# Products with the weights' upper part first in every 3-pass tile, those with the lower part last

## The reference

```
for l in range(DEPTH):                                   # DEPTH = 2
    u = rms_norm(x, mix_norm_g[l]) @ w_in[l]             # one input projection, split among three groups
    y_mla = mla_group(...)                               # latent attention, 8 heads, causal
    y_ssm = mamba2_group(...)                            # state-space scan in chunks of 128
    y_lru = rglru_group(...)                             # gated linear recurrence
    y_mix = concat([rms_norm(y_mla), y_ssm, rms_norm(y_lru)])
    x = x + y_mix @ w_out[l]
    x = x + memory_cross_attention(rms_norm(x), rms_norm(mem), w_mq[l], w_mk[l], w_mv[l], w_mo[l])
    hm = rms_norm(x, mlp_norm_g[l]) @ w_mlp1[l]          # 1024 -> 4096
    x = x + jnp.square(jax.nn.relu(hm)) @ w_mlp2[l]      # 4096 -> 1024
return rms_norm(x, final_norm_g)
```

## Time and profile before

| what | value |
|---|---|
| median of 3 runs | 3390.11 us (3389.93 to 3394.16) |
| the profiled execution | 3385.11 us |
| its span, first to last instruction | 3383.4 us |
| PE busy | 3054.3 us, 90% of the span, 14184 matmuls |
| POOL busy | 1143.3 us, 34% |
| DVE busy | 1212.6 us, 36% |
| ACT busy | 702.3 us, 21% |
| mean granted TensorE clock | 0.97 of full speed |

### The profile page before, as it was taken

One profiled execution on the slowest core, in us unless ns is written; L12 is line 12 of the kernel. 1 busy time (PEld: TensorE's weight loads), 2 busy tenths in 40 slices (PEclk: granted clock), 3 DMA queues, 4 the chain that ended last, 5 costly groups with the idle time before them and its releaser, 6 DMA issues. The chain is left out here.

```text
span 3383.4 us, 35420 instructions
## 1 busy us (share of the span) xinstructions
PE 3054.3 (90%) x14184; PEld 2404.3 (71%) x14184; DVE 1212.6 (36%) x1195; ACT 702.3 (21%) x1143; POOL 1143.3 (34%) x598
## 2 busy tenths in 40 slices
PE   4888899989999999999878889998889999999996
PEld 3765557766678888888767555687668788888885
DVE  6365445303432222222254644451044222222223
ACT  3034552103211001010121345420031111111011
POOL 2221213562233334343233122235603334334341
PEclk8889999999999999999988899999999999999998
DMA  3000001121011111111110000111201111111111
GB/s 131 31 23 12 5 1 63 56 75 43 31 38 50 44 50 43 50 49 44 40 42 31 20 6 1 38 44 63 81 13 43 38 50 43 50 50 43 50 48 58
DMA packets 41927, 142.88 MB, mean 42 GB/s; under 512 B 7024, under 2 KB 9072, under 8 KB 41200
## 3 DMA queue, kind: packets, MB, share of 16 engines
q1 hardware_dynamic: 41840, 141.67, 12.4%
HBM read 135.89 MB, written 5.77 MB: 42 GB/s over the span
## 5 line engine op out<-in xcount | busy, mean ns | idle before, releaser
L474 POOL TENSOR_TENSOR wsp<-raw,ones 128x1024 fp32r<-128x1024 f32 x236 | 453.0, 1919 | 1688.7 <-PE ps L602 1620.7
L602 PE MATMUL ps<-hB,wsp 128*128 128x512 f32 x3840 | 875.6, 389 | 5.4 <-DVE hB L1451 3.3
L602 PEld LDWEIGHTS ps<-hB,wsp 128*128 128x128 f32 x3840 | 720.8, 188 | 156.4 <-ACT hB L1119 4.1
L602 PE MATMUL ps<-hA,wsp 128*128 128x512 f32 x2880 | 672.6, 395 | 61.0 <-POOL wsp L477 44.7
L602 PE MATMUL ps<-hm,wsp 128*128 128x512 f32 x3072 | 703.2, 390 | 26.6 <-DVE hm L1537 26.6
L602 PEld LDWEIGHTS ps<-hm,wsp 128*128 128x128 f32 x3072 | 575.3, 188 | 151.8 <-issue 32.9
L602 PEld LDWEIGHTS ps<-hA,wsp 128*128 128x128 f32 x2880 | 547.8, 191 | 184.2 <-POOL wsp L477 39.3
L477 POOL TENSOR_TENSOR wsp<-raw,wsp 128x1024 fp32r<-128x1024 f32 x236 | 575.4, 2438 | 18.5
L1547 DVE TENSOR_TENSOR x<-ps,x 128x1024 f32<-128x1024 f32 x128 | 156.7, 1224 | 501.1 <-PE ps L602 501.1
L1181 ACT ACTIVATE ss<-ss 128x1024 f32<-128x1024 f32 x32 | 34.0, 1062 | 918.6 <-DVE ss L1529 918.6
L763 PE MATMUL ps<-kT,qT 96*128 96x512 f32 (+3 forms) x384 | 147.8, 494 | 25.8 <-POOL qT L510 14.7
(11 more groups left out here) (259 smaller groups left out, 2548.5 us busy)
## 6 DMA issues: line engine op xcount, KB each, us to landing
raw<-in_weight_tiles SPq DMA_DIRECT2D x236, 512.0 KB, 3.3
x<-in_xT SPq DMA_DIRECT2D x1, 4096.0 KB, 14.7
outT<-x SPq DMA_DIRECT2D x8, 512.0 KB, 3.1
wh<-in_head_weights SPq DMA_DIRECT2D x8, 256.0 KB, 2.7
mem_s<-memory_normed SPq DMA_DIRECT2D x2, 1024.0 KB, 5.0
memp<-in_memT SPq DMA_DIRECT2D x1, 1024.0 KB, 4.9
memory_normed<-memp SPq DMA_DIRECT2D x1, 1024.0 KB, 4.1
pos_i<-in_positions SPq DMA_DIRECT2D x1, 512.0 KB, 5.4
```

The costliest lines, as they stand in the source:

```text
L474: pool.tensor_tensor(wsp[:, s, 0, :], raw[:, s, :], ones[:, 0:1].to_broadcast([P, TILE]), ALU.mult).then_inc(w_ready[s], 1)
L602: last = pe.matmul(ps[:, 2 * buf + half, 0:n], w[:, k, col:col + P], rhs(part, k, half * n, n), start=(at_k == 0 and w is w_hi and part == 0),
```

## The change

`tile3` is given the round r and makes the waits for the weights itself. It first waits for the upper part (`w_ready >= 2r+1`) and issues, for all chunks, the four matmuls with `w_hi`. Then it waits for the lower part (`2r+2`) and issues, for all chunks, the two with `w_lo`. The hooks stay at the chunks of the first group. `memory_values` is regrouped in the same way. The waits for both parts ahead of the tiles are gone. The number of matmuls, their operands and POOL's program are the same.

```diff
-                    def tile3(s, buf, rhs, nk=DC, col=0, width=TILE // DC, cols=T, hooks=None, order=None):
+                    def tile3(s, buf, rhs, r, nk=DC, col=0, width=TILE // DC, cols=T, hooks=None, order=None):
...
-                        for at_k, k in enumerate(order or range(nk)):
+                        ks = order or range(nk)
+                        pe.wait_ge(w_ready[s], r * 2 + 1)
+                        for at_k, k in enumerate(ks):
                             if hooks:
                                 hooks(at_k)
-                            for w, part in ((w_hi, 0), (w_hi, 1), (w_lo, 0)):
+                            for part in range(2):
                                 for half in range(cols // n):
-                                    last = pe.matmul(ps[:, 2 * buf + half, 0:n], w[:, k, col:col + P],
-                                                     rhs(part, k, half * n, n),
-                                                     start=(at_k == 0 and w is w_hi and part == 0),
-                                                     stop=(at_k == nk - 1 and w is w_lo))
+                                    pe.matmul(ps[:, 2 * buf + half, 0:n], w_hi[:, k, col:col + P],
+                                              rhs(part, k, half * n, n), start=(at_k == 0 and part == 0), stop=False)
+                        pe.wait_ge(w_ready[s], r * 2 + 2)
+                        for at_k, k in enumerate(ks):
+                            for half in range(cols // n):
+                                last = pe.matmul(ps[:, 2 * buf + half, 0:n], w_lo[:, k, col:col + P],
+                                                 rhs(0, k, half * n, n), start=False, stop=(at_k == nk - 1))
...
                         for s in range(2):
-                            pe.wait_ge(w_ready[s], r * 2 + 2)
                             pe.wait_ge(t_free[s], u + 1)
-                            tile3(s, s, rhs, cols=cols, hooks=hooks if s == 0 else None, order=order).then_inc(t_ready[s], 1)
+                            tile3(s, s, rhs, r, cols=cols, hooks=hooks if s == 0 else None, order=order).then_inc(t_ready[s], 1)
...
                         for s in range(2):
-                            pe.wait_ge(w_ready[s], r * 2 + 2)
                             w = wsp[:, s, :, :].rearrange("p a (k m) -> p a k m", m=HT)
-                            for k in range(2):
-                                for a, b in ((0, 0), (1, 0), (0, 1)):
+                            for b, parts in ((0, (0, 1)), (1, (0,))):
+                                pe.wait_ge(w_ready[s], r * 2 + 1 + b)
+                                for k, a in ((k, a) for k in range(2) for a in parts):
...
                             s = j % 2
-                            pe.wait_ge(w_ready[s], (b * 4 + 2 + j // 2 + R_MLP) * 2 + 2)
                             for m in range(2):
                                 pe.wait_ge(t_free[m], b * 6 + 2 + j + U_MLP + 1)
-                                tile3(s, m, of(hm), nk=4, col=m * P, width=2 * P,
+                                tile3(s, m, of(hm), b * 4 + 2 + j // 2 + R_MLP, nk=4, col=m * P, width=2 * P,
```

## The result

The changed kernel took 3426.66 us in the median of 4 executions (3424.03 to 3429.63), the kernel before 3390.02 us beside it (3388.40 to 3394.16). The ratio is 1.0106 [1.0089, 1.0124], so it is slower by about 36 us. The profiled execution took 3424.06 us, 38.95 more than the one before, and its span is 3422.3 us. The forecast was slower, 3411.9 us in a range from 3395 to 3428. The sign holds and so does the range, by 1.3 us; the term for the clock is too small.

The account below looks back on a forecast made before the run. TensorE, busy 90% of the span, was taken to bound the kernel. Terms -18.6 + 0 + 21.8 + 5.0 + 13.6 = +21.8 us on a 3390.1 us median gave 3411.9 us, range 3395 to 3428.

Parts of the forecast that it names:

- the term for the clock: Feed-forward blocks: longer waits let TensorE's clock fall in 8 of 16 blocks, 1.7 us each, +13.6 us.
- Part 1: Memory stage: PE need not wait for the weights' lower part, 9.3 us saved per layer, -18.6 us in all.
- the middle link: Memory stage: the last value tile ends 4.3 us earlier, so POOL's waiting split and its chain come 4.3 us early.
- Part 2: Layer start: a later end hides in the 9.1 us wait for DVE's sum; price 0, 1 us either way.
- Part 3: Lower products come after the last activation chunk: feed-forward blocks +21.8 us, output projection +5.0, memory stage's first tile 0.
- The first query tile: First tile of the memory stage: no wait from the new order, price 0, with 0.6 us to spare.
- the waits in mid-tile: The added wait within each tile: priced at 0, with 0.02 us for some 200 tiles, 4 us, in the range.
- Part 4: Feed-forward blocks: `hm` waits growing from 1.67 to 3.03 us bring clock falls, +13.6 us, bounds 0 and 27.
- so I take half of them: Feed-forward blocks: a clock fall at half of the sixteen lengthened waits, 8 x 1.7 = +13.6 us.
- The price of a fall: Work lost when TensorE's clock falls behind a wait: 4.00 x 0.43 = 1.7 us each.
- Rival B: Feed-forward: a clock fall at every block, +27.2 us for the clock, +35.4 in all, 3425.5 us; chance 0.18.

Follow-up runs that it names:

- Experiment 2: Kernel before, with the new order only in tiles that wait for no activation chunks (tiles without hooks): 3373.09 us, ratio 0.9948 to the kernel before.
- Experiment 9: Experiment 2 with the memory stage's value tiles in the old order, one wait for both weight parts: 3379.44 us, ratio 0.9963 to the kernel before.
- experiments 5 to 7: Changed kernel with three, four and five dummy matmuls ahead of the wait for the last `hm` chunk: 3420.29, 3422.16 and 3418.19 us.
- experiment 10: Experiment 2 with the first two tiles on `hm` of each feed-forward block interleaved: 3342.80 us, ratio 0.9859 to the kernel before.

## Why the prediction was right and wrong

**Part 1, the memory stage: right.** Experiment 2 measures 8.7 us per layer for it alone (9.3 forecast), 17.4 in both stages. The steps in the changed kernel, at the three query pairs, were -0.7, -4.1 and -2.3 us in layer 0 and -1.9, -4.1 and -2.3 in layer 1, where 2.5, 4.3 and 2.5 were followed. Experiment 9 shows the middle link: with the value tiles as before the idle row of POOL is as long as before. What is missing in layer 0 is mostly the clock over the first key pair. That the fall there lasted longer is seen, why it did was not tried.

**Part 2, the start of a layer: right in its mechanism, with a shift of its own in layer 0.** The later end of the pair is hidden: the wait ahead of the statistics fell from 9.1 to 3.65 us (6.7 forecast), and they began 1.0 us earlier in layer 0 (67.68 against 68.69), not at the same moment. Whether the stage's +2.8 us is the change's the runs don't tell: in the six kernels with the new order there it is between +0.8 and +3.4, in the five others with the old one between 0.0 and +2.6 (experiment 9).

**Part 3, work behind the last chunk: right, to 0.02 us in the feed-forward blocks.** 1.34 us per block against 1.36, a wait of 2.99 against 3.03. The output projection took 3.6 and 3.7 us more against 2.5: the work behind the last chunk is the 2.5, and the fall of the clock behind this wait, 1.1 us in each layer, has no term in the prediction. The first query tile cost nothing. That the waits in mid-tile are free holds too: a feed-forward block of experiment 2 has eleven such waits and takes 88.97 us, as before.

**Part 4, the clock: the step that failed is "so I take half of them".** The price of a fall was right (1.58 against 1.7), the number was not: thirteen, not eight, and one of them long. With 12 x 1.58 + 2.8 = 21.8 us in place of 13.6, the sum would have been +30.0. The rest of the 38.95 are the layer starts and attention (+3.1), the output projection (+2.3), the memory stages (+3.3 less gain) and small remainders. The medians lie closer together than the profiled executions, 36.6 us, so the forecast missed them by 14.8. I took half because a middling wait seemed to bring a fall by chance and because the matmuls round these waits are dense. Neither holds: the dense matmuls didn't keep the clock up in thirteen of sixteen blocks, and experiments 5 to 7 show hardly any slope between 1.88 and 2.99 us. What I could have read: of the two like waits of 1.85 us one already had a fall, and 3.03 us lay well beyond it. Rival B, a fall at every block (3425.5 us), is the closest to the measured median, although three blocks kept their clock. That is in part luck: its 27.2 us for the clock are 5.4 too many, and the terms named above that came out dearer fill the difference. The range holds the median only because it was drawn to take in rival B. Why a spared block follows where the walk passes 1.5 us was not tried.

The Trainium skill (TensorE: Matmul & The Clock Gate, "Loop structure matters more than you think") says that the clock falls ahead of each burst when PE waits long between bursts. By that rule part 4 would have been 16 falls; this case's runs give 11 to 13 of 16 at waits from 1.88 to 2.99 us and none at 1.67, so the trace agrees for most blocks.

## What to carry to other kernels

Reordering a reduction is a matter of what stands in front of the last wait: where operands arrive late, put all work that doesn't need them there (another tile's too, experiment 10), and use an order by the weights' part only in tiles whose activations are complete. A loop that repeats a short wait of TensorE may stand just below a clock fall: here 0.2 us more of waiting (1.67 to 1.88) cost another 1.6 us in eleven turns of sixteen. So price a lengthened wait with its falls in most turns, at every place where it grows, and try a filler or a delay on the chip before believing a halfway figure.

## What the runs showed of the hardware that was not expected

**Idle TensorE time can be dearer than work.** 96 dummy matmuls made the changed kernel 24.6 us faster, since they shortened sixteen waits from 2.99 to 1.67 us.

**A tiny DVE instruction held for 2 us beside POOL.** At the start of layer 0 after the change:

```profile
66.56 3.20 POOL L477 TENSOR_TENSOR wsp<-raw,wsp 128x1024 fp32r<-128x1024 f32 x1
...
67.71 2.09 DVE L1229 TENSOR_SCALAR spt<-sm 128x2 f32<-128x2 f32 x1
```

The same instruction took 0.17 us before. It ends at 69.80, POOL's at 69.76, and POOL's own 3.20 us are long against 2.35 elsewhere. The chain of small instructions behind it came about 1 us later. Before the change a split of 3.21 us at 61.87 stood beside an addition of DVE that took 2.10 us instead of 1.23. The Trainium skill (SBUF — State Buffer, "SBUF: two separate sides") says that VectorE and GpSimd lock each other out of one pair of ports for a whole instruction, if VectorE's has two inputs in SBUF or runs in a mode that uses two ports. That the short one ends 0.04 us after the long one agrees with it; whether this small instruction is of such a kind no run shows. It wasn't tried by an experiment.
